# The last six expert units in another order, with the pair tokens gathered earlier and the round count made first

## Chip, cores and metric

The kernel runs on one core of one Trainium2 chip. The metric is the device time of one execution in microseconds. Before the change the median of three runs is 901.22 us (901.0 to 903.43).

## What is computed

One inference step of a two-layer decoder trunk for 288 tokens (256 of a prompt, 32 of running sequences), model width 1024. Layer 0 ends in a dense feed-forward block, layer 1 in a mixture of experts, and only the latter is touched here:

```python
logits = (x @ w_router) + b_router
top_v, top_i = lax.top_k(logits, 2)              # 2 of 8 experts for each token
top_w = jax.nn.softmax(top_v, axis=-1)
gates = sum of one_hot(top_i, 8) * top_w
for e in range(8):
    out = out + gates[..., e:e+1] * swiglu(x, we_gate[e], we_up[e], we_down[e])
# swiglu(x, wg, wu, wd) = (silu(x @ wg) * (x @ wu)) @ wd ; wg, wu: 1024 x 1376, wd: 1376 x 1024
```

## The kernel before, in words

The queue of SyncE (SP) brings the expert weights in. TensorE (PE) multiplies, ScalarE (ACT), VectorE (DVE) and GpSimd (POOL) prepare the operands. Every engine has its own program, written out by hand, and they meet at semaphores.

**Units and steps.** The router counts the tokens of each expert, and the kernel sorts the experts by that count. A *wide* unit is one expert with up to 128 tokens; a *pair* unit is two experts with up to 64 tokens each, side by side. A unit has 27 steps in the order of `STEPS`: eight `up` steps (128 rows of the up matrix each), `gate` 0 to 2 of the **next** unit, eleven `down` steps (the last has 96 rows), then `gate` 3 to 7 of the next unit. The first unit's eight `gate` steps stand ahead of everything (the *lead*, `LEAD = 8`), and the last unit has no gate steps (`LAST_STEPS`). Steps are numbered n = 0, 1, 2, ... through the whole stage.

**Buffers.** Step n uses slot n % 9 (`NSLOT = 9`), so SP may start the load of step n when PE has finished step n - 9 (`w_used`). A slot holds one chunk of a wide step (128 x 1376 or 128 x 1024 fp32) or both chunks of a pair step, which are twice the bytes.

**Wide and pair steps.** A wide chunk is split before use: ACT rounds it to a high half (`moe_high`, L931, five steps ahead of PE), DVE or POOL subtracts that from the raw chunk to get the low half (`moe_low`, four steps ahead; L1699 is DVE's `tensor_tensor`, L757 POOL's), and PE does three passes (L1498, L1499, L1501; for down L1609, L1610, L1613). A pair chunk is used raw, in fp32 (L1514, L1527); ACT and DVE do nothing to it.

**Rounds.** A loop (`Fori(0, more)`) does two wide units a round; `more` is 1 when no expert has over 128 tokens and no later one over 64, else 6. Here it is 1. Behind the loop stand two wide units, then two pair units: in all wide, wide, wide, wide, pair, pair. In this document they are units 0 to 5. `more` comes from `ni_sb`, computed on DVE from the sorted counts; SP, PE, ACT and POOL wait for it (`ni_ready`) before the loop. SP needs it ahead of the load of step 9.

**The lead on DVE.** After the token tables and the gathers' low halves, DVE does `lead_low(r)` and `moe_low` of steps 0 to 3, then the expert ids for the later rounds, the sorted counts and `ni_sb`, then the rest. POOL does `moe_low` of steps 4 and 6 (`POOL_LEAD`).

**Gathers and scatters.** PE gathers tokens into unit order with one-hot matmuls (L1486 to L1489, ten of them for a piece, four pieces). Unit 0 gathers for the next two wide units, unit 2 for all pairs, both between down steps 4 to 9. The results of a unit are scattered back with matmuls (L1544, L1545) between its last gate steps, and DVE adds them to x (L1699 on `xb`).

```python
TOK_ORDER = (2, 4, 0, 3, 5, 1)
NSLOT = 9
STEPS = ([("up", k) for k in range(KT)] + [("gate", 0), ("gate", 1), ("gate", 2)]
         + [("down", k) for k in range(FT)] + [("gate", k) for k in range(3, KT)])
```

Of the kernel before, what the change touches and what calls it, by code (L numbers as in the profile page):

```python
# [15 lines left out]
P = 128  # L16
# [20 lines left out]
FT = 11  # L37
# [54 lines left out]
LEAD_BANK = (3, 5, 4, 6)  # L92
FILL_MASK, FILL_TOK = 11, 6
# [10 lines left out]
SMALL_FROM = LEAD + PER  # L104
POOL_STEPS = (12, 15, 18, 21, 25)
POOL_LEAD = (4, 6)
# [51 lines left out]
def step_of(n):  # L158

    return ("gate", n) if n < LEAD else STEPS[(n - LEAD) % PER]  # L160
# [12 lines left out]
def build(nc, x_d, consts_d, cols_d, misc_d, w_in_d, w_out_d, b_d, c_d, glu_d, ln_d, wst_d, wss_d,  # L173
# [3 lines left out]
    with ctx:  # L177
# [143 lines left out]
        pair_x = [hb[:, 0:1024].rearrange("p (k s) -> p k s", k=KT), stage]  # L321
# [246 lines left out]

        def wait_halves(eng, n, i=None, final=False):
# [12 lines left out]
        def _(sp):  # L582
# [97 lines left out]
            def load_expert_chunk(e, row, n, i=None):  # L680

                r, w = extent(step_of(n))
                if n >= NSLOT:
                    sp.wait_ge(w_used, upto(i, 2 * PER, n - NSLOT + 1))
                sp.dma_start(raw_half(n)[0:r, 0:w], source(e, row, step_of(n))).then_inc(w_in_slot[n % NSLOT], 16)

            def load_small_chunks(experts, step, n, i):

                r, w = extent(step)
                sp.wait_ge(w_used, upto(i, 2 * PER, n - NSLOT + 1))  # L690
                for (e, row), dst in zip(experts, raw_pair(n)):
                    sp.dma_start(dst[0:r, 0:w], source(e, row, step)).then_inc(w_in_slot[n % NSLOT], 16)  # L692
# [16 lines left out]
            def load_pair(i, final):  # L709

                experts = [expert_at(bass.ds(i * 2 + e, 1)) for e in range(2 if final else 3)]
                for n in range(NSLOT, NSLOT + 2 * PER if not final else LEAD + 2 * PER):
                    if final and small_step(n):
                        load_small_chunks(pairs[0], step_of(n), n, i)
                    else:
                        load_expert_chunk(*experts[(n - LEAD) // PER + (step_of(n)[0] == "gate")], n, i)

            with sp.Fori(0, more) as i:
                load_pair(i, False)
            pairs = [[expert_at(slice(4 + 2 * u + g, 5 + 2 * u + g)) for g in range(2)] for u in range(2)]  # L720
            load_pair(more, True)
            n = LEAD + 2 * PER
            for u, steps in enumerate((STEPS, LAST_STEPS)):
                for step in steps:
                    load_small_chunks(pairs[u + (step[0] == "gate")], step, n, more)
                    n += 1
# [8 lines left out]
        def _(pool):  # L735
# [16 lines left out]
            def moe_low(n, i=None, final=False):  # L752

                r, w = extent(step_of(n))
# [124 lines left out]
            for n in POOL_LEAD:  # L879
                moe_low(n)  # L880
# [3 lines left out]
            def pair(i, final):  # L884

                for n in range(LEAD + LOW_AHEAD, LEAD + 2 * PER + (0 if final else LOW_AHEAD)):
                    if moe_by_pool(n) and not (final and small_step(n)):
                        moe_low(n, i, final)

            with pool.Fori(0, more) as i:  # L890
                pair(i, False)
            pair(more, True)
# [14 lines left out]
        def _(act):  # L907
# [19 lines left out]
            def moe_high(n, i=None, final=False):  # L927

                r, w = extent(step_of(n))
# [205 lines left out]

            def one(i, a, final):

                n0 = LEAD + PER * a
                d0 = STEPS.index(("down", 0))
                for q in range(PER):  # L1140
                    if q == 0:
                        gate_silu(i, a, n0)
                    if q == KT and a == 1 and not final:
                        act.wait_ge(w_used, upto(i, 2 * PER, n0 + KT))
                        act.activation(hg_h[1], stage, ACT.Copy).then_inc(hgbh_ready, 1)
                    if q == d0 - 1:
                        hidden_rows(i, a, het_h)
                    if a == 0 and q - d0 in (5, 6, 9, 10):
# [3 lines left out]
                        act.activation((pair_x[0] if final else hg_h[0])[:, 2 * r:2 * r + 2, :],  # L1152
# [3 lines left out]
                    for n in range(n0 + q + ACT_AHEAD - (q == d0 + FT), n0 + q + ACT_AHEAD + (q != d0 + FT - 1)):  # L1156
                        if not (final and small_step(n)):
                            moe_high(n, i, final)

            def pair_unit(i, a, last):  # L1160

                n0, steps = LEAD + PER * a, LAST_STEPS if last else STEPS
                d0 = steps.index(("down", 0))
                gate_silu(i, a, n0)
                hidden_rows(i, a, pair_het)
                output_act(i, a, n0 + d0 + FT)
# [12 lines left out]
            for a in range(2):  # L1179
                one(more, a, True)  # L1180
            for a in (2, 3):
                pair_unit(more, a, a == 3)
# [12 lines left out]
        def _(pe):  # L1195
# [271 lines left out]
            for u, (_, w) in enumerate(TILES):  # L1467
                mm = pe.matmul(ps[:, 7, 24:32], ones[0:w, :], mask[0:w, u, :], start=(u == 0), stop=(u == 2))
# [62 lines left out]
            def scatter(k, i, a, gathers, final=False):  # L1531

                if k == 0:
                    pe.wait_ge(sgt_ready, each(i, a, 1, 1))
                    pe.wait_ge(yel_ready, each(i, a, 2, 1))
                    if gathers:
                        pe.wait_ge(hgh_ready if final else hgl_ready, i * 4 + 8)
# [38 lines left out]
            def one(i, a, final):  # L1576

                n0 = LEAD + PER * a
                gathers = a == 0

                for q, (kind, k) in enumerate(STEPS):
                    if q == 0:
                        pe.wait_ge(xadd, each(i, a, 8, X_MOE - 8 + 3))
                        if a == 0:
                            pe.wait_ge(hgbl_ready, i + 1)
                    if kind == "up":
# [850 lines left out]
```

## Time and profile before

| what | value |
|---|---|
| median of three runs | 901.22 us (901.0 to 903.43) |
| the profiled execution's own time | 900.76 us |
| its span in the trace | 898.9 us |
| mean granted TensorE clock | 0.98 |
| PE, DVE, ACT, POOL busy | 828.6, 561.3, 391.6, 256.3 us |
| HBM read | 197.20 MB |

The trace's times are microseconds from the start of the span, and the profiled execution takes 1.86 us more than its span. The mixture of experts begins at about 490 us and holds the rest of the span. Busy time of PE is modelled: a matmul's record is longer than the distance to the next one, so distances between starts are used for rates.

### The profile page before, as it was taken

To read this page: it belongs to the slowest core of one execution; us is meant where nothing else is said; L and a number is where in the kernel's file an instruction comes from. 1 tells how busy PE (TensorE), PEld (TensorE's weight loads), DVE (VectorE), ACT (ScalarE), POOL (GpSimd) and SP (SyncE) were. 2 spreads that over 40 slices of the span, in tenths; PEclk is the share of its full clock that TensorE was granted. 3 is DMA by queue.
4 is the path that set the end of the run, shared out by engine and by line. 5 is a ranking of instruction groups with operands and counts; after the bars stand their busy time and mean duration, and the time that the engine had idled before them with its cause. 6 is when DMAs were issued, how large, how long until landed. Compare 5 with 4: busy or idle time off the path is not lost.

```text
span 898.9 us, 13791 instructions
## 1 busy us (share of the span) xinstructions
PE 828.6 (92%) x5116; PEld 642.6 (71%) x5116; DVE 561.3 (62%) x978; ACT 391.6 (44%) x574; POOL 256.3 (29%) x208
## 2 busy tenths in 40 slices
PE   9699899999989999999999878999999998868774
PEld 8368679999989999668778766888888652313222
DVE  7959867566955665579733879799987631102004
ACT  5186344455323440486322647767867410001002
POOL 7762124222425540551111205214061320000003
PEclk9989999999999999999999799999999999999998
DMA  9500814655655521820500768999989999999991
GB/s 300 175 1 4 301 58 129 217 167 158 179 142 135 175 72 48 233 104 4 196 1 1 282 260 297 340 312 320 387 291 339 344 406 421 420 374 422 420 390 62
DMA packets 87634, 199.71 MB, mean 222 GB/s; under 512 B 25984, under 2 KB 47728, under 8 KB 87568
## 3 DMA queue, kind: packets, MB, share of 16 engines
q1 hardware_dynamic: 86768, 197.81, 61.8%
q8 instruction: 41, 0.67, 0.3%
q10 hardware_dynamic: 576, 0.59, 0.2%
q0 software_dynamic: 224, 0.43, 0.1%
q14 instruction: 25, 0.20, 0.1%
HBM read 197.20 MB, written 1.61 MB: 221 GB/s over the span
## 4 chain that ended last, share of the span: by engine, by line
PE 56%; DVE 18%; SPq 9%; DMA 7%; issue 5%; ACT 3%; POOL 1%; DVEq 0%; ACTq 0%; POOLq 0%
SPq L692 8%; PE ps L1213 6%; PE ps L1212 6%; PE ps L1214 6%; PE ps L1396 5%; DVE D L1699 4%; DMA wraw_g<-in_moe_w_up 3%; PE ps L1258 3%; PE ps L1501 2%; PE ps L1499 2%; PE ps L1498 2%; DMA wraw_u<-in_moe_w_up 2%; DVE M L1699 2%; PE ps L1609 2%; PE ps L1610 2%
## 5 line engine op out<-in xcount | busy, mean ns | idle before, releaser
L1212 PE MATMUL ps<-Md,split_u 128*128 128x288 f32 (+2 forms) x304 | 89.7, 295 | 0.0
L1214 PE MATMUL ps<-Md,split_u 128*128 128x288 f32 (+2 forms) x304 | 89.1, 293 | 0.0
L931 ACT ACTIVATE wrnd_g<-wraw_g 128x1376 fp32r<-128x1376 f32 (+2 forms) x50 | 60.2, 1214 | 46.0 <-DMA wraw_g<-in_moe_w_down 29.2
L1699 DVE TENSOR_TENSOR xb<-xb,ps 128x288 f32<-128x288 f32 x80 | 33.2, 450 | 67.9 <-PE ps L1396 29.1
L1699 DVE TENSOR_TENSOR wrnd_g<-wraw_g,wrnd_g 128x1376 fp32r<-128x1376 f32 (+1 forms) x42 | 63.0, 1524 | 14.6 <-ACT wrnd_g L931 14.4
L1699 DVE TENSOR_TENSOR wrnd_u<-wraw_u,wrnd_u 128x1376 fp32r<-128x1376 f32 (+1 forms) x38 | 67.7, 1813 | 2.5 <-ACT wrnd_u L931 2.4
L757 POOL TENSOR_TENSOR wrnd_g<-wraw_g,wrnd_g 128x1024 fp32r<-128x1024 f32 (+1 forms) x8 | 29.0, 3631 | 120.0 <-ACT wrnd_g L931 120.0
L763 POOL TENSOR_TENSOR hb<-hb 128x288 f32<-128x288 f32 x11 | 8.7, 795 | 183.3 <-ACT hb L912 182.8
L931 ACT ACTIVATE wrnd_u<-wraw_u 128x1376 fp32r<-128x1376 f32 (+1 forms) x47 | 56.8, 1258 | 3.4 <-DMA wraw_u<-in_moe_w_gate 2.8
L1213 PE MATMUL ps<-hbr,split_u 128*128 128x288 f32 (+1 forms) x192 | 57.1, 297 | 0.0
L1214 PEld LDWEIGHTS ps<-Md,split_u 128*128 128x128 f32 (+2 forms) x304 | 56.9, 187 | 0.0
L1212 PEld LDWEIGHTS ps<-Md,split_u 128*128 128x128 f32 (+2 forms) x304 | 56.8, 187 | 0.1
L925 ACT ACTIVATE split_u<-raw 128x1024 fp32r<-128x1024 f32 (+2 forms) x38 | 39.6, 1048 | 36.4 <-PE ps L1214 36.4
L1699 DVE TENSOR_TENSOR split_u<-raw,split_u 128x1024 fp32r<-128x1024 f32 (+2 forms) x28 | 39.4, 1414 | 19.4 <-ACT split_u L925 19.3
L749 POOL TENSOR_TENSOR split_d<-raw,split_d 128x1024 fp32r<-128x1024 f32 (+1 forms) x9 | 21.4, 2379 | 98.7 <-ACT split_d L925 98.7
L1396 PE MATMUL ps<-D 128*128 128x288 f32 x192 | 48.4, 409 | 0.0
L1212 PE MATMUL ps<-Md,split_d 128*128 128x288 f32 (+1 forms) x144 | 43.4, 301 | 3.9 <-DVE xb L1699 2.8
L1699 DVE TENSOR_TENSOR M<-M,ps 64x256 f32<-64x256 f32 (+3 forms) x38 | 18.3, 504 | 44.0 <-PE ps L1514 43.7
L2186 DVE SCALAR_TENSOR_TENSOR Me<-ps,M,Me 128x512 fp32r<-128x512 f32 x12 | 8.4, 746 | 59.6 <-ACT Me L1173 59.6
L1214 PE MATMUL ps<-Md,split_d 128*128 128x288 f32 (+1 forms) x144 | 42.9, 298 | 0.0
L1396 PEld LDWEIGHTS ps<-D 128*128 128x128 f32 x192 | 36.0, 190 | 9.4
L757 POOL TENSOR_TENSOR wrnd_u<-wraw_u,wrnd_u 128x1376 fp32r<-128x1376 f32 (+1 forms) x9 | 29.4, 3268 | 45.2 <-ACT wrnd_u L931 45.2
(425 smaller groups left out, 2242.8 us busy)
## 6 DMA issues: line engine op xcount, KB each, us to landing
wraw_u<-in_moe_w_gate SPq DMA_DIRECT2D x39, 688.0 KB, 9.2
wraw_g<-in_moe_w_up SPq DMA_DIRECT2D x32, 688.0 KB, 12.9
wraw_g<-in_moe_w_down SPq DMA_DIRECT2D x38, 512.0 KB, 9.3
wraw_u<-in_moe_w_down SPq DMA_DIRECT2D x34, 512.0 KB, 14.0
wraw_u<-in_moe_w_up SPq DMA_DIRECT2D x24, 688.0 KB, 15.1
wraw_g<-in_moe_w_gate SPq DMA_DIRECT2D x18, 688.0 KB, 6.6
raw<-in_ffn_w_gate SPq DMA_DIRECT2D x20, 512.0 KB, 4.5
raw<-in_ffn_w_up SPq DMA_DIRECT2D x20, 512.0 KB, 4.3
```

The lines of the kernel that those rows point to most:

```text
L692: sp.dma_start(dst[0:r, 0:w], source(e, row, step)).then_inc(w_in_slot[n % NSLOT], 16)
L749: pool.tensor_tensor(lo[0:r, 0:w], raw_slot(n)[0:r, 0:w], hi[0:r, 0:w].bitcast(F32), ALU.subtract).then_inc(lo_pool, 1)
L757: pool.tensor_tensor(lo[0:r, 0:w], raw_half(n)[0:r, 0:w], hi[0:r, 0:w].bitcast(F32), ALU.subtract).then_inc(w_lo_pool, 1)
L925: act.activation(split_slot(n)[0][0:r, 0:w], raw_slot(n)[0:r, 0:w], ACT.Copy).then_inc(hi_done, 1)
L931: act.activation(halves(n)[0][0:r, 0:w], raw_half(n)[0:r, 0:w], ACT.Copy).then_inc(w_hi, 1)
L1212: pe.matmul(out, w_hi, x_hi, start=start, stop=False)
L1213: pe.matmul(out, w_hi, x_lo, start=False, stop=False)
L1214: return pe.matmul(out, w_lo, x_hi, start=False, stop=stop)
L1258: mm = pe.matmul(ps[0:n, 4 + t, :], h[:, k, t0:t0 + n], w_in[:, k, 2 * MIX:IN_W], start=(k == 0), stop=(k == KT - 1))
L1396: mm = pe.matmul(bank(out_bank[m]), w_out[:, k, m * P:(m + 1) * P], yn(k), start=(m >= 4 and k == 0), stop=(k == (MT - 1 if m < 4 else KT ...
L1498: pe.matmul(o, hg_h[hg][:, k, :], w_hi[:, f0:f1], start=(k == 0), stop=False)
L1699: return dve.tensor_tensor(o, a, b, op)
```

## The change

Four things change together.

1. The final part is wide, pair, wide, pair in place of wide, wide, pair, pair. With the loop's two wide units the whole is wide, wide, wide, pair, wide, pair. The same chunks are loaded and multiplied, in another order.
2. The pairs' tokens are gathered in unit 2 beside up steps 2 to 5, into banks 6, 7, 0, 1, in place of beside its down steps; their one-hots are made on DVE at that unit's start in place of at its fourth step. The buffer `pair_x[0]` moves.
3. The ids of the first experts are made before the first two token tables, and the later ids, the sorted counts and `ni_sb` before `lead_low(0)`.
4. POOL has no steps of the lead any more: DVE does `moe_low` 4 and 6 too, and the position and gate tables come after steps 8 and 9.

```diff
+PAIR_BANK = (6, 7, 0, 1)
-SMALL_FROM = LEAD + PER
+UNITS = 4
+TOTAL = LEAD + (UNITS - 1) * PER + len(LAST_STEPS)
-POOL_LEAD = (4, 6)
...
-    return n in POOL_LEAD if n < LEAD else (n - LEAD) % PER in POOL_STEPS
+    return n >= LEAD and (n - LEAD) % PER in POOL_STEPS
...
-    return n >= SMALL_FROM and (n >= SMALL_FROM + PER or STEPS[(n - LEAD) % PER][0] == "gate")
+    if n < LEAD:
+        return False
+    a = min((n - LEAD) // PER, UNITS - 1)
+    return (a + (step_of(n, True)[0] == "gate")) % 2 == 1
...
-        pair_x = [hb[:, 0:1024].rearrange("p (k s) -> p k s", k=KT), stage]
+        pair_x = [D[:, 3456:4480].rearrange("p (k s) -> p k s", k=KT), stage]
...
+            def pair_tokens(i, r):
+
+                act.wait_ge(gather_mm, i * 4 + 4 + r + 1)
+                both = ps[:, PAIR_BANK[r], :].rearrange("p (k s) -> p k s", s=2 * P)
+                act.activation(pair_x[0][:, 2 * r:2 * r + 2, :], both[:, :, 0:P], ACT.Copy)
+                act.activation(pair_x[1][:, 2 * r:2 * r + 2, :], both[:, :, P:2 * P], ACT.Copy).then_inc(hgh_ready, 1)
...
-                    pe.matmul(bank(0, P), ones, ones, start=True, stop=True)
+                    pe.matmul(ps[64:128, 1, 0:P], ones[:, 0:64], ones, start=True, stop=True)
...
+                    if final and a == 0 and q - 2 in range(4):
+                        if q == 2:
+                            pe.wait_ge(oh_ready, i + 2)
+                            pe.wait_ge(xadd, each(i, a, 8, X_MOE))
+                        elif q == 4:
+                            pe.wait_ge(esilu_ready, each(i, a, 3, 3))
+                        gather(q - 2, PAIR_BANK[q - 2])
...
-            token_low(0)
-            token_low(1)
             dve.wait_ge(tot_mm, 1)
-            dve.wait_ge(pos_mm, 1)
...
             dve.tensor_copy(ids_sb[:, 0:NE], idf).then_inc(ids_ready, 1)
+            token_low(0)
+            token_low(1)
+            dve.wait_ge(pos_mm, 1)
...
-            for r in range(3):
-                lead_low(r)
-                if not moe_by_pool(r):
-                    moe_low(r)
-            lead_low(3).then_inc(hgbl_ready, 1)
-            moe_low(3)
+            dve.wait_ge(e_ready, 1)
             dve.tensor_copy(ids_sb[:, 8:12], idf[:, 0:4]).then_inc(ids_ready, 1)
...
             dve.tensor_scalar(ni_sb[:, :], cn[:, 2:3], float(MORE), 1.0, ALU.mult, ALU.add).then_inc(ni_ready, 1)
+            for r in range(3):
+                lead_low(r)
+                if not moe_by_pool(r):
+                    moe_low(r)
+            lead_low(3).then_inc(hgbl_ready, 1)
+            moe_low(3)
...
-                    if q == 3 and a == 0:
+                    if a == 0 and q == (0 if final else 3):
```

**Place 1, DVE in the lead.** Before, the round count stands behind the four first chunks (`hbr`, `hgb` are the halves of the gathered tokens, `wrnd_g` a low half, `ids_sb` the expert ids, `ni_sb` the round count):

```order
L2128 SCALAR_TENSOR_TENSOR Me<-ps,G,Me 32x512 [waits tokh_ready]
L1699 TENSOR_TENSOR hbr<-ps,hbr 128x256 [waits hgh_ready]
L1699 TENSOR_TENSOR hgb<-ps,hgb 128x256
L1699 TENSOR_TENSOR wrnd_g<-wraw_g,wrnd_g 128x1376 [waits w_hi]
...
L1699 TENSOR_TENSOR wrnd_g<-wraw_g,wrnd_g 128x1376 [waits w_hi]
L2212 CAST ids_sb<-G 128x4
L2213 CAST ids_sb<-G 128x2
L1699 TENSOR_TENSOR G<-G 128x64
L2215 TENSOR_REDUCE G<-G 128x8 [waits dve_chain]
L2216 TENSOR_SCALAR G<-G 128x1 [waits dve_chain]
L2217 TENSOR_SCALAR G<-G 128x1
L1699 TENSOR_TENSOR G<-G 128x1 [waits dve_chain]
L2219 TENSOR_SCALAR ni_sb<-G 128x1 [waits dve_chain]
```

With the change the same eight instructions stand ahead of the first `hbr`, and the low halves of steps 4 to 8 follow each other:

```order
L2124 SCALAR_TENSOR_TENSOR Me<-ps,G,Me 32x512 [waits tokh_ready]
L2203 CAST ids_sb<-G 128x4 [waits e_ready]
L2204 CAST ids_sb<-G 128x2
L1695 TENSOR_TENSOR G<-G 128x64
L2206 TENSOR_REDUCE G<-G 128x8 [waits dve_chain]
L2207 TENSOR_SCALAR G<-G 128x1 [waits dve_chain]
L2208 TENSOR_SCALAR G<-G 128x1
L1695 TENSOR_TENSOR G<-G 128x1 [waits dve_chain]
L2210 TENSOR_SCALAR ni_sb<-G 128x1 [waits dve_chain]
L1695 TENSOR_TENSOR hbr<-ps,hbr 128x256 [waits hgh_ready]
...
L1695 TENSOR_TENSOR wrnd_u<-wraw_u,wrnd_u 128x1376 [waits w_hi] x4
```

Eight instructions moved past four chunks' low halves and the halves of the gathered tokens, and two low halves (of steps 4 and 6) came to DVE from POOL.

**Place 2, PE in unit 2.** The first wide unit behind the loop, its third up step. Before, it follows the second directly, and nothing but weights is waited for:

```order
L1501 MATMUL ps<-wrnd_g,hbr 128x512 x2
L1501 MATMUL ps<-wrnd_g,hbr 128x352
L572 REGISTER_ALU
L1498 MATMUL ps<-wrnd_g,hbr 128x512 [waits w_lo_dve]
L1499 MATMUL ps<-wrnd_g,hbr 128x512
```

With the change a piece of the gather (`Me` holds the tokens and their one-hots) stands between, and waits for DVE's one-hots and for the last additions to x:

```order
L1507 MATMUL ps<-wrnd_g,hbr 128x352
L1596 REGISTER_ALU
L1597 REGISTER_ALU [waits oh_ready]
L1492 MATMUL ps<-Me 128x256 [waits xadd]
L1493 MATMUL ps<-Me 128x256
L1492 MATMUL ps<-Me 128x256
L1493 MATMUL ps<-Me 128x256
L1495 MATMUL ps<-Me 128x256
```

Four such pieces moved from the down steps to up steps 2 to 5, with a wait for `oh_ready` two steps into the unit. The twelve one-hots it waits for are on DVE:

```order
L1695 TENSOR_TENSOR wrnd_g<-wraw_g,wrnd_g 128x1376 [waits w_hi]
L2316 REGISTER_ALU
L2316 COMPARE_AND_BRANCH
L2266 ISA
L2158 TENSOR_SCALAR Me<-consts,G 128x64 [waits gather_mm]
L2158 TENSOR_SCALAR Me<-consts,G 128x64 x11
```

They stood three low halves later before, and now follow the low half of that unit's fourth up step.

**Place 3, SP's loads behind the loop.** Before, unit 2's gate steps are the next wide expert's (one chunk a step, L685); the program reads, from unit 2's last up chunk on:

```order
L685 DMA wraw_u<-in_moe_w_up 128x1376
...
L685 DMA wraw_u<-in_moe_w_gate 128x1376
...
L685 DMA wraw_d<-in_moe_w_gate 128x1376
...
L685 DMA wraw_g<-in_moe_w_gate 128x1376
```

With the change they are the first pair's, two chunks a step (L705):

```order
L697 DMA wraw_u<-in_moe_w_up 128x1376
...
L705 DMA wraw_u<-in_moe_w_gate 128x1376
...
L705 DMA wraw_u<-in_moe_w_gate 128x1376
...
L705 DMA wraw_d<-in_moe_w_gate 128x1376
...
L705 DMA wraw_d<-in_moe_w_gate 128x1376
```

So the double-sized loads begin one unit earlier, and a wide expert's single ones stand among them later.

## Rows read from the trace of the kernel before

**Rows 1.** The page: busy time of PE; DMA share in 40 slices of the span

```profile
PE 828.6 (92%) x5116; PEld 642.6 (71%) x5116; DVE 561.3 (62%) x978; ACT 391.6 (44%) x574; POOL 256.3 (29%) x208
DMA  9500814655655521820500768999989999999991
```

**Rows 2.** Timeline of SP's queue, 495 to 525: start, us, queue, line, operation

```profile
502.64 0.38 SPq L685 DMA_DIRECT2D wraw_d<-in_moe_w_up  x1
522.52 2.49 SPq L685 DMA_DIRECT2D wraw_g<-in_moe_w_up  x3
```

**Rows 3.** Timeline of DVE, 505 to 600, in the lead

```profile
510.89 1.58 DVE L1699 TENSOR_TENSOR wrnd_g<-wraw_g,wrnd_g 128x1376 fp32r<-128x1376 f32 x1
512.39 3.13 DVE L2212 CAST ids_sb<-G 128x4 int32<-128x4 f32 x1
...
515.50 3.18 DVE L1699 TENSOR_TENSOR G<-G 128x64 f32<-128x64 f32 x1
...
519.41 0.15 DVE L2219 TENSOR_SCALAR ni_sb<-G 128x1 int32<-128x1 f32 x1
```

**Rows 4.** Timeline of POOL, 505 to 600, its two chunks of the lead

```profile
511.45 7.14 POOL L757 TENSOR_TENSOR wrnd_u<-wraw_u,wrnd_u 128x1376 fp32r<-128x1376 f32 x2 [20.81 <-ACT wrnd_u L931]
```

**Rows 5.** Timeline of PE, 508 to 560: lead and unit 0; brackets: idle before, releaser

```profile
512.79 0.39 PE L1498 MATMUL ps<-wrnd_g,hbr 128*128 128x512 f32 x1
...
521.88 0.50 PE L1498 MATMUL ps<-wrnd_u,hbr 128*128 128x512 f32 x1 [4.14 <-DVE wrnd_u L1699]
...
529.17 0.39 PE L1498 MATMUL ps<-wrnd_d,hbr 128*128 128x512 f32 x1
...
534.14 0.50 PE L1498 MATMUL ps<-wrnd_g,hbr 128*128 128x512 f32 x1 [1.08 <-DVE wrnd_g L1699]
...
541.50 0.50 PE L1498 MATMUL ps<-wrnd_u,hbr 128*128 128x512 f32 x1 [1.46 <-DVE wrnd_u L1699]
...
552.69 1.58 PE L1565 MATMUL ps<-consts,M 128*128 128x128 f32 x11 [1.09 <-DVE M L1699]
554.03 0.48 PE L1498 MATMUL ps<-wrnd_g,hgb 128*128 128x512 f32 x1
```

**Rows 6.** Windows: stretch, length, busy times, granted clock, DMA share, GB/s

```profile
522.00:525.00 3.00, 3.00 (x9) 2.49 (x10) 2.76 (x11) 0.00 (x0) 0.00 (x0) 0.56 0.48 128
637.10:691.20 54.10, 54.04 (x282) 46.39 (x281) 46.07 (x57) 39.69 (x46) 17.09 (x5) 1.00 0.93 333
745.60:826.80 81.20, 66.03 (x311) 21.73 (x311) 8.92 (x22) 4.49 (x11) 0.00 (x0) 1.00 1.02 407
800.00:806.00 6.00, 3.59 (x16) 0.77 (x12) 0.00 (x0) 0.00 (x0) 0.00 (x0) 1.00 1.05 256
826.00:860.00 34.00, 28.13 (x138) 9.80 (x138) 4.79 (x13) 2.93 (x7) 0.00 (x0) 1.00 1.02 421
```

**Rows 7.** Timeline of PE: starts of steps in units 0, 2 and 3

```profile
566.12 0.28 PE L1486 MATMUL ps<-Me 128*128 128x256 f32 x1
...
567.30 0.39 PE L1609 MATMUL ps<-wrnd_u,Me 128*128 128x512 f32 x1
...
637.14 0.39 PE L1498 MATMUL ps<-wrnd_d,hbr 128*128 128x512 f32 x1
...
639.01 0.39 PE L1498 MATMUL ps<-wrnd_g,hbr 128*128 128x512 f32 x1
...
691.23 0.39 PE L1498 MATMUL ps<-wrnd_d,hgb 128*128 128x512 f32 x1
...
714.84 0.50 PE L1609 MATMUL ps<-wrnd_g,Me 128*128 128x512 f32 x1
```

**Rows 8.** Timeline of DVE, 626 to 662, around the start of unit 2

```profile
638.51 0.81 DVE L1699 TENSOR_TENSOR xb<-xb,ps 128x288 f32<-128x288 f32 x2
...
645.25 2.04 DVE L2162 TENSOR_SCALAR Me<-consts,G 128x64 fp32r<-128x64 f32 x12
```

**Rows 9.** Timeline, 875 to 900: the last down step and the first scatter

```profile
879.55 2.50 PE L1527 MATMUL ps<-wraw_d,M 96*64 96x512 f32 x8
```

More of the change, by code:

```diff
@@ L707, in _ @@
             more = loops(sp)
[L709 to L716, printed above, removed]
             with sp.Fori(0, more) as i:
-                load_pair(i, False)
+                experts = [expert_at(bass.ds(i * 2 + e, 1)) for e in range(3)]
+                for n in range(NSLOT, NSLOT + 2 * PER):
+                    load_expert_chunk(*experts[(n - LEAD) // PER + (step_of(n)[0] == "gate")], n, i)
+            wide = [expert_at(bass.ds(more * 2 + e, 1)) for e in range(2)]
             pairs = [[expert_at(slice(4 + 2 * u + g, 5 + 2 * u + g)) for g in range(2)] for u in range(2)]
[L721 to L726, printed above, removed]
+            for n in range(NSLOT, TOTAL):
+                a = (n - LEAD) // PER if n < TOTAL - len(LAST_STEPS) else UNITS - 1
+                a += step_of(n, True)[0] == "gate"
+                if a % 2:
+                    load_small_chunks(pairs[a // 2], n, more)
+                else:
+                    load_expert_chunk(*wide[a // 2], n, more, True)
             for k in range(KT):
@@ L878, in _ @@
             pool.wait_ge(tokz_ready, 1)
-            for n in POOL_LEAD:
-                moe_low(n)
             pool.wait_ge(ni_ready, 1)
             more = loops(pool)
[L884 to L888, printed above, removed]
             with pool.Fori(0, more) as i:
-                pair(i, False)
-            pair(more, True)
+                for n in range(LEAD + LOW_AHEAD, LEAD + 2 * PER + LOW_AHEAD):
+                    if moe_by_pool(n):
+                        moe_low(n, i)
+            for n in range(LEAD + LOW_AHEAD, TOTAL):
+                if moe_by_pool(n) and not small_step(n):
+                    moe_low(n, more, True)
             for k in range(1, 4):
@@ L1156, in one @@
                     for n in range(n0 + q + ACT_AHEAD - (q == d0 + FT), n0 + q + ACT_AHEAD + (q != d0 + FT - 1)):
-                        if not (final and small_step(n)):
+                        if not (final and (n >= TOTAL or small_step(n))):
                             moe_high(n, i, final)
[L1160 to L1166, printed above, removed]
+                if len(steps) == d0 + FT:
+                    output_act(i, a, n0 + len(steps))
             def output_act(i, a, used):
@@ L2268, in one @@
                 n0 = LEAD + PER * a
-                d0 = STEPS.index(("down", 0))
-                for q in range(PER):
-                    if q == 3 and a == 0:
+                small, last = final and a % 2 == 1, final and a == UNITS - 1
+                steps = LAST_STEPS if last else STEPS
+                d0 = steps.index(("down", 0))
+                for q in range(len(steps)):
+                    if a == 0 and q == (0 if final else 3):
                         dve.wait_ge(gather_mm, i * 4 + 4)
@@ L2283, in one @@
                         tt(hg_l[1], stage, hg_h[1].bitcast(F32), ALU.subtract).then_inc(hgbl_ready, 1)
-                    if q == d0 - 1:
+                    if q == d0 - 1 and not small:
                         for b in range(3):
@@ L2306, in one @@
                         output_dve(i, a)
-                    if STEPS[q][0] == "gate" and STEPS[q][1] in ADD_AT:
-                        j = 2 * ADD_AT.index(STEPS[q][1])
+                    if steps[q][0] == "gate" and steps[q][1] in ADD_AT:
+                        j = 2 * ADD_AT.index(steps[q][1])
                         for m in (j, j + 1):
```

176 lines of the change are left out of this document (81 added, 95 removed).

## The prediction

> **What bounds the kernel now.** I read the page first. PE is busy 92% of the span, so an average says "PE". The slices say otherwise: DMA share is 8 or 9 from the 25th slice to the last but one, and has a hole at the 21st and 22nd, about where the experts begin [rows 1]. So I took windows, unit by unit [rows 6]. Unit 2, wide, lasts 54.1 us with PE busy 54.0: PE sets the pace, and the queue moves 333 GB/s. Unit 4, a pair, lasts 81.2 us with PE busy 66.0 while DMA share is above 1 at 407 GB/s: the loads set the pace. Where loads run undisturbed they give 421 GB/s (826 to 860) [rows 6]; that is my rate for a full queue. The two kinds of unit have opposite bounds, and nine slots let the queue run nine steps ahead, no more.
>
> Then SP's timeline at the hole: the last of the nine free-slot loads is issued at 502.64, the next at 522.52 [rows 2]. It waits neither for a slot nor for PE: it waits for the round count, which DVE writes at 519.41 [rows 3]. On DVE a cast of 128x4 takes 3.13 us and a 128x64 operation 3.18 us, next to 0.15 us for an operation of like size; POOL's two chunks of the lead run from 511.45 to 518.59, over both [rows 3, 4]. PE idles 4.14 us until 521.88, then has granted clock 0.56 until 525 [rows 5, 6].
>
> **Part 1: the round count and the lead.** The eight instructions go ahead of `lead_low(0)`. Without POOL beside them they are small: from 518.59, where POOL lets go, to 519.56 DVE does five of them, and with two casts of about 0.15 and the 128x64 operation I put them at 1.4 us. DVE had waited there for ACT anyway, so I price them at 0, and at 1.4 for the high end, if that cover is gone.
>
> The low halves then follow each other at 1.50 us (510.89 to 512.39 [rows 3]). Low 3 ends at 512.4; lows 4 to 8, two of them POOL's before, end at 513.9, 515.4, 516.9, 518.4 and 519.9. PE starts step 3 at 512.79 [rows 5] and takes 1.87 us a wide step (637.14 to 639.01 [rows 7]): steps 4 to 7 at 514.66, 516.53, 518.40, 520.27, and unit 0's first up step at 522.14. Each low half is there before. In the trace that step starts at 529.17 [rows 5]: **7.0 us** earlier. The load of step 9 goes out when PE has finished step 0, near 509, not at 522.52, so it is not late.
>
> Up to gate 2 of unit 0 the trace has more waits (1.08, 1.46, 1.09 and smaller ones): 554.03 - 529.17 = 24.9 us for ten wide steps and the transposes, 18.7 + 1.3 = 20.0 at full pace [rows 5]. Some of these 4.9 us go too, as their cause was the late loads. But the position and gate tables, some twenty small instructions (an estimate at 0.15 us each: 3 us), now run on DVE between lows 8 and 10, and DVE at 1.50 us a chunk has only 0.37 us of slack a step. I count 0 here, with -1.5 and +2 as ends. Making the ids ahead of the first two token tables starts the very first loads a little earlier; PE is then at the gathers, so 0.
>
> A rule of the Trainium skill bears on POOL's part. The trace: 3.13 and 3.18 us under POOL, 0.15 us without [rows 3, 4]. SBUF — State Buffer, section "Who interferes with whom", says that DVE and GpSimd share one port pair as an exclusive lock held for a whole instruction, and that casts and two-input operations in SBUF fall under it. By the rule as by the rows the two waits (6 us) vanish; the sum above does not use it, as it counts from each low's end.
>
> **Part 2: the order of units.** I count what the queue still has to load from a point where it becomes continuously busy. At 421 GB/s: wide up or gate (128 x 1376 fp32, 0.7045 MB) 1.67 us, wide down 1.25, pair up or gate 3.35, pair down 2.49. A 96-row pair chunk costs 1.87 plus what the dip at 800 to 806 loses: 256 GB/s for 6 us is 6 x (1 - 256/421) = 2.35 us [rows 6], so 4.2. For a wide one I take 2.1.
>
> While PE does down steps, the queue loads, nine steps ahead, the next gates and ups. Before, these first become pair chunks in unit 3; from its first down step at 714.84 [rows 7] the queue has no more rest. Left then: unit 3: one down, the 96-row one, five pair gates = 20.1; unit 4: 8 up, 3 gate, 10 down, 96-row, 5 gate, all pair = 26.8 + 10.05 + 24.9 + 4.2 + 16.75 = 82.7; unit 5: 26.8 + 24.9 + 4.2 = 55.9. Sum 158.7, end at 873.5. (Landing and PE's last steps bring the last down step to 879.55 [rows 9]; that offset of 6 us is the same after.)
>
> After, the same point comes in unit 2. Unit 2 starts at 637.14. To its first down step it now does what unit 3 does (wide ups, pair gates, 714.84 - 691.23 = 23.6 us), plus four gather pieces of 1.18 us (566.12 to 567.30), 4.7 us, which its down steps lose [rows 7]. Plus a new wait, named next. Left then: 20.1; unit 3 (pair ups, wide gates, pair downs) 26.8 + 5.0 + 24.9 + 4.2 + 8.35 = 69.3; unit 4 (wide ups, pair gates, wide downs) 13.4 + 10.05 + 12.5 + 2.1 + 16.75 = 54.8; unit 5 55.9. Sum 200.1.
>
> *The new wait.* PE wants the one-hots at unit 2's third step, 637.14 + 2 x 1.87 = 640.9. DVE does the last additions to x at 638.51 (0.81), a low half (1.5), then the twelve one-hots (2.04 [rows 8]), and is done at 642.8. PE waits **1.9 us**; behind it on PE stand all up steps, and all wait. Before, the one-hots ran at 645.25, with no one waiting. If DVE is later there, 3 us; if PE is later anyway, 0.
>
> So the point is at 637.14 + 23.6 + 4.7 + 1.9 = 667.4, and the end at 667.4 + 200.1 = 867.5: **6.0 us** ahead of 873.5. Put otherwise: the old order let the queue idle through one more wide unit. Does it really stay busy? It would stop if it got nine steps ahead. In the new unit 4, PE's work and the loads are nearly alike (ups 15.0 to 13.4, pair gates 8.8 to 10.0, downs 15.6 to 14.6); PE enters it some 7 us behind (first wide chunk after a pair one goes through ACT and DVE, about 3 us; five wide gates with scatters, 11.4 us of PE for 8.4 of loads). 8 us of lead is at most six chunks. It holds, with little to spare: I give this term 3 to 8 us.
>
> **Sum.** 7.0 + 6.0 = 13.0 us off 900.76 us of the profiled execution (span 898.9) gives 887.8 us; the median 901.22 stands 0.5 us above that execution, so I forecast **888.2 us**. Part 4 of the change, the moved buffer and the filler matmuls of 64 columns, moves no work: 0.
>
> **Rivals.**
> - *Only the lead gains.* The wide units behind pair units are late for the split, PE falls back, and the slots fill, so that the queue idles as before. For it: the thin margin in unit 4. Against it: PE's idle share in unit 4 of before, 15 of 81 us [rows 6]. Time: 900.8 - 7.0 + 0.5 = 894.2. Chance 0.12.
> - *Only the order gains.* In unit 0 DVE becomes the bound (two more lows, the tables, the loop's own one-hots) and gives back the 7 us before the loop's second unit. Time 895.2. For it: DVE's waits in rows 5 are of that kind. Against it: POOL no longer holds it for 6 us. Chance 0.08.
> - *Nothing of either* (a load elsewhere is the true bound): 0.04, within 0.3% of 901.2.
> - *Slower: PE loses its clock.* The row: after 4.14 us of idling, clock 0.56 (the 1.2 GHz level, for most of 3 us) [rows 5, 6]. The new order has a place with two waits close together, at the end of unit 3's downs: about 2 us for the 96-row chunk, then about 3 us for the first split. If the clock fell there and at the like places, and pair steps then ran at 1.2 GHz, a pair step would take 4.9 us of PE for 3.35 us of loads: 1.5 us lost a step, and from nine such steps on the 13 us are gone; all 16 up steps of units 3 and 5 would give 888.2 + 24 = 912. Against it: clock 1.00 all through unit 4 of before, at waits of 0.8 us a step [rows 6]. Chance 0.04. The Trainium skill speaks for it: TensorE: Matmul & The Clock Gate, section "HAM oscillation", tells of a kernel that waits for DMA between short bursts and is throttled again at each. The 1.00 of unit 4 does not bear that out for waits this short.
> - My forecast: 0.72.
>
> **Range.** The bounds: 5.5 to 9 us for the lead, 3 to 8 for the order, so 884.2 to 892.7 for the likeliest case alone; with both one-sided rivals, **884.0 to 895.3**. Faster by over 0.3%: 0.92; within 0.3% (what a measurement of this kernel can tell from no change): 0.04; slower: 0.04.
>
> **What would show it.** `ni_sb` written near 503 on DVE; SP's tenth load near 509; first up step near 522; no granted clock below 0.9 between 510 and 875; a PE wait of 1.9 us for DVE's one-hots near 634; loads at about 421 GB/s with no gap from about 660; in unit 3 a wait of 2 to 3 us at the first wide gate; the last down step near 866.5. I am wrong if the queue has gaps in the last 200 us, if DVE is ahead of PE by nothing in unit 0, or if PE's clock drops at unit 3's end.

## The result

The changed kernel takes **892.61 us** (median of four runs, 891.37 to 894.31) against 901.14 us (901.0 to 903.43) for the kernel before, run beside it: a ratio of 0.9901 with a 95% interval of 0.9878 to 0.9923. That is 8.5 us or 1.0% faster. I had forecast 888.2 us, a gain of 13.0. The time lies inside the range of 884.0 to 895.3, but a third of the gain is missing.

The profiled execution took 892.68 us, its span is 890.9 us. From its page, PE's busy time and clock and the DMA share in 40 slices; they answer to [rows 1]:

```profile
PE 827.4 (93%) x5116; PEld 643.5 (72%) x5116; DVE 559.9 (63%) x980; ACT 391.4 (44%) x574; POOL 243.9 (27%) x206
PEclk9889999999999999999999699999999999999998
DMA  9500723755554521830500697989979999989991
```

Each slice is 22.3 us. Behind the hole, the 24th slice (512 to 535 us) now has a DMA share of 9 in place of 6. But the 36th (780 to 802 us) has an 8 inside the last stretch of nines, where I had expected no gap. And PE's clock is 0.6 in the 23rd (490 to 512 us), where it was 0.7.

The lead, on SP's timeline (answers to [rows 2]) and DVE's (answers to [rows 3]):

```profile
501.87 0.39 SPq L697 DMA_DIRECT2D wraw_d<-in_moe_w_up  x1
510.59 5.92 SPq L697 DMA_DIRECT2D wraw_g<-in_moe_w_up  x4
```

```profile
503.03 0.17 DVE L2203 CAST ids_sb<-G 128x4 int32<-128x4 f32 x1
...
503.18 0.22 DVE L1695 TENSOR_TENSOR G<-G 128x64 f32<-128x64 f32 x1
...
504.12 0.15 DVE L2210 TENSOR_SCALAR ni_sb<-G 128x1 int32<-128x1 f32 x1
...
513.31 6.09 DVE L1695 TENSOR_TENSOR wrnd_u<-wraw_u,wrnd_u 128x1376 fp32r<-128x1376 f32 x4
```

`ni_sb` is written at 504.12 in place of 519.41, the cast takes 0.17 us in place of 3.13, and SP's tenth load goes out at 510.59 in place of 522.52. Now PE's timeline; the rows are the first filler group, the first up step of unit 0, the transposes, unit 2's start, the new wait for the one-hots, unit 2's first down step, and the last down step (they answer to [rows 5, 7, 9]):

```profile
489.42 4.28 PE L1469 MATMUL ps<-ones_r 128*64 128x128 f32 x22
...
523.32 0.39 PE L1504 MATMUL ps<-wrnd_d,hbr 128*128 128x512 f32 x1
...
544.78 1.58 PE L1571 MATMUL ps<-consts,M 128*128 128x128 f32 x11 [1.09 <-DVE M L1695]
...
628.91 0.39 PE L1504 MATMUL ps<-wrnd_d,hbr 128*128 128x512 f32 x1
...
634.68 0.38 PE L1492 MATMUL ps<-Me 128*128 128x256 f32 x1 [1.87 <-DVE Me L2158]
...
659.46 0.50 PE L1633 MATMUL ps<-wrnd_g,Me 128*128 128x512 f32 x1
...
872.09 1.89 PE L1533 MATMUL ps<-wraw_d,M 96*64 96x512 f32 x8
```

Read it from the two ends. Unit 2 starts 8.2 us earlier than before (628.91 against 637.14 [rows 7]). The last down step starts 7.5 us earlier (872.09 against 879.55 [rows 9]), and the span is 8.0 us shorter. So **all of the gain is there when unit 2 starts, and the order, which acts from there on, brought nothing** in this execution. My sum had 7.0 us for the lead and 6.0 for the order.

Where the order's 6 us went shows in the windows (stretch, length, busy times of PE, PEld, DVE, ACT, POOL, granted clock, DMA share, GB/s):

```profile
740.00:750.00 10.00, 7.15 (x26) 1.90 (x24) 0.00 (x0) 0.02 (x1) 0.00 (x0) 0.83 1.03 289
780.00:790.00 10.00, 10.00 (x55) 4.53 (x54) 7.58 (x10) 8.01 (x11) 3.73 (x2) 1.00 0.85 326
790.00:800.00 10.00, 10.00 (x46) 8.17 (x45) 9.61 (x7) 4.59 (x5) 5.03 (x3) 1.00 0.89 293
800.00:810.00 10.00, 10.00 (x48) 5.65 (x47) 1.41 (x2) 1.26 (x2) 1.88 (x1) 1.00 1.02 420
```

The 289 GB/s at 740 is the 96-row pair chunk that I had priced. The 326 and 293 are new: against 420 they are (94 + 127) / 42 = 5.3 us of a resting queue, in unit 4. What it waits for stands on SP's and PE's timelines:

```profile
785.64 0.33 SPq L697 DMA_DIRECT2D wraw_d<-in_moe_w_down  x1
789.45 0.33 SPq L697 DMA_DIRECT2D wraw_g<-in_moe_w_down  x1
```

```profile
786.74 2.53 PE L1520 MATMUL ps<-wraw_g,D 128*64 128x512 f32 x12
789.20 0.50 PE L1633 MATMUL ps<-wrnd_g,Me 128*128 128x512 f32 x1
```

Down load 8 goes out at 789.45, when PE has finished gate 2 (786.74 to 789.20), whose slot it takes. The queue is nine steps ahead, and issues nothing for 3.5 us.

### The profile page after: what moved, and what is told of

It is laid out like the page before. It is cut to its first block, busy times and chain, and to the rows that moved or that the text cites. A ratio compares the mean times of both kernels' runs of the same rounds, so it can differ in the third digit from the quotient of the medians.

```text
span 890.9 us, 13793 instructions
## 1 busy us (share of the span) xinstructions
PE 827.4 (93%) x5116; PEld 643.5 (72%) x5116; DVE 559.9 (63%) x980; ACT 391.4 (44%) x574; POOL 243.9 (27%) x206
## 4 chain that ended last, share of the span: by engine, by line
PE 63%; DVE 15%; DMA 6%; ACT 5%; issue 5%; SPq 4%; POOL 1%; DVEq 0%; ACTq 0%; POOLq 0%
PE ps L1219 6%; PE ps L1218 6%; PE ps L1220 6%; PE ps L1402 5%; SPq L705 4%; PE ps L1520 4%; DMA wraw_u<-in_moe_w_gate 4%; DVE D L1695 3%; PE ps L1507 3%; PE ps L1505 3%; PE ps L1504 3%; PE ps L1633 2%; PE ps L1634 2%; PE ps L1637 2%; DVE M L1695 2%
## 5 line engine op out<-in xcount | busy, mean ns | idle before, releaser
L1695 DVE TENSOR_TENSOR wrnd_u<-wraw_u,wrnd_u 128x1376 fp32r<-128x1376 f32 (+1 forms) x40 | 72.2, 1838 | 25.6 <-ACT wrnd_u L935 25.4
L765 POOL TENSOR_TENSOR wrnd_g<-wraw_g,wrnd_g 128x1024 fp32r<-128x1024 f32 (+1 forms) x8 | 23.5, 2942 | 136.6 <-ACT wrnd_g L935 136.6
L1219 PE MATMUL ps<-hbr,split_u 128*128 128x288 f32 (+1 forms) x192 | 57.1, 297 | 0.0
L765 POOL TENSOR_TENSOR wrnd_u<-wraw_u,wrnd_u 128x1024 fp32r<-128x1024 f32 (+1 forms) x7 | 22.1, 3163 | 116.7 <-ACT wrnd_u L935 116.7
L1520 PE MATMUL ps<-wraw_u,D 128*64 128x512 f32 (+1 forms) x192 | 40.4, 555 | 5.0 <-DMA wraw_u<-in_moe_w_up 5.0
L1219 PEld LDWEIGHTS ps<-hbr,split_u 128*128 128x128 f32 (+1 forms) x192 | 35.9, 187 | 0.1
```

The costliest lines, as they stand in the source:

```text
L765: pool.tensor_tensor(lo[0:r, 0:w], raw_half(n)[0:r, 0:w], hi[0:r, 0:w].bitcast(F32), ALU.subtract).then_inc(w_lo_pool, 1)
L1219: pe.matmul(out, w_hi, x_lo, start=False, stop=False)
L1520: mm = pe.matmul(ps[own, b0 + b, 0:f1 - f0], pair_x[u][:, k, own], w[g][:, f0:f1], start=(k == 0), stop=(k == KT - 1))
L1695: return dve.tensor_tensor(o, a, b, op)
```

## The experiments

Twelve kernels ran, in three sets of four, each set on one chip with the kernel before beside it (medians 900.96, 901.79 and 901.5 us). Single executions of one kernel differ by 5 us and more, so beside each median I give the ratio to the kernel before, and in the traces I compare stretches.

### The order alone, the lead alone

```diff
 # e1_order_only: the changed kernel, its lead taken back
+            for n in POOL_LEAD:
+                moe_low(n)
...
+            lead_low(3).then_inc(hgbl_ready, 1)
+            moe_low(3)
             dve.tensor_copy(ids_sb[:, 8:12], idf[:, 0:4]).then_inc(ids_ready, 1)
 # e2_lead_only: the kernel before, with the changed lead (no lows on POOL); units and pairs as they were
```

> The changed kernel with the lead of the kernel before: round count after the lows, POOL_LEAD lows, 128-column filler matmuls. So this is the order alone. Theory A (the order is worth nothing and the lead all): from the start of unit 2 on both kernels took the same time (244.9 and 245.1 us), so this run ties with the kernel before, 901 us (899 to 903), unit 2 starts near 637 us of its span and the last down step some 242.5 us later. Theory B (my prediction's: the order is worth 6 us less the 0 that the lead lost): 895 us. In both the profile should show SP's load of step 9 late again, near 522 us.

> The kernel before, its units in their old order, with the new lead: round count, number casts and one-hots made before the lows, no lows on POOL in the lead, and the 64-column filler matmuls with the total in bank 0. Theory A: the lead is worth the 8.2 us that unit 2 starts earlier in the changed kernel, and the old order keeps them: 893 us (891.5 to 894.5), the same as the changed kernel. Theory B: 7.0 us of 13 come from the lead, and the order's share was then eaten by something else that the changed order brought: also near 893 us if the lead is 8 us, so it is the run of the order alone that tells the two apart; above 897 us both theories are wrong, since then lead and order need each other.

Order alone: 899.6 us (897.92 to 903.13, twelve runs), ratio 0.9983 (0.9958 to 1.0007). Lead alone: 893.1 us (891.37 to 895.82), ratio 0.9899 (0.9857 to 0.9941), as fast as both together. Theory A (the lead is all) holds, theory B (6 us of order) falls: the interval leaves the order at most 3.8 us and is centred on 1.5. In the profile of the order alone SP's tenth load is late again (525.60, in an execution that came to the fillers 2.7 us later than the kernel before), TensorE waits the same 1.87 us for the one-hots, and the queue rests in unit 4 as well, at 312 and 286 GB/s in two windows of 10 us, 5.8 us.

### Which part of the lead

Two parts of the new lead can be had alone: the early round count with POOL's lows kept (L1's candidate), and POOL's two lows given to DVE with the count left where it was (L2's).

```diff
 # e5_count_early: kernel before, DVE's part and the second filler group as changed, but
             for n in range(4, LEAD + LOW_AHEAD):
-                moe_low(n)
+                if not moe_by_pool(n):
+                    moe_low(n)
 # e6_no_pool_lead: kernel before, one line
-POOL_LEAD = (4, 6)
+POOL_LEAD = ()
```

> The kernel before, in its old order, with the round count and the one-hots early as in the changed kernel, but POOL keeps its two lows of the lead (steps 4 and 6, 7.14 us for both). Theory L1 (the round count's place gives the 8 us: it is out before POOL starts its lows, so nothing waits behind them): SP's next load near 511 us in place of 522.5, and 893.5 us. Theory L2 (the lows on POOL cost by themselves, since VectorE's small operations or TensorE's steps 4 and 6 wait for them wherever the count stands): not under 896 us.

> The kernel before with POOL's two lows of the lead given to VectorE and nothing else: the round count stays behind the lows of steps 0 to 3. Its casts then take 0.2 us in place of 3.13 and 3.18 us, the count is out at 513.6 us of the span in place of 519.4, SP's next load is at 516.7 us in place of 522.5, and the first up step, which waited 4.14 us, is bound by TensorE's own queue of work: 5.8 us of the queue's delay gone, of which 4.1 us reach the end. Forecast 896.8 us by theory L1. By theory L2 it gives nearly all of the 8: 893 us.

Count early: 894.67 us, ratio 0.993 (0.9907 to 0.9953); SP's next load goes out at 507.51. That is nearer to L1's 893.5 than to L2's "not under 896". No lows on POOL: 894.82 us, ratio 0.9921 (0.9901 to 0.9941). Each alone brings 6 to 7 us, both 8 to 9: they remove the same stall, and are not to be added. My price for the second, 896.8 us, was wrong: I took 4.1 us as all that the path could give. But with the casts at 0.17 us DVE does its lows of the lead earlier too, and PE had been waiting for those [rows 5]. From the totals' matmuls to unit 0's transposes the profiles give 60.3 us before, 53.6 with the count early, 51.4 without POOL's lows, 51.2 for the changed kernel and 51.1 for the lead alone. The lead alone is the early count without POOL's lows, so POOL's lows cost 2.5 us of the stretch where the count is early (53.6 to 51.1), and once they are gone the early count adds 0.3 us (51.4 to 51.1), which is less than profiles differ by: the nine with the changed lead give 49.0 to 51.3. First DVE with the count early, then POOL in the same stretch:

```profile
509.41 1.58 DVE L1700 TENSOR_TENSOR wrnd_g<-wraw_g,wrnd_g 128x1376 fp32r<-128x1376 f32 x1
510.91 9.01 DVE L1700 TENSOR_TENSOR wrnd_u<-wraw_u,wrnd_u 128x1376 fp32r<-128x1376 f32 x2
519.85 1.58 DVE L1700 TENSOR_TENSOR wrnd_d<-wraw_d,wrnd_d 128x1376 fp32r<-128x1376 f32 x1
```

```profile
509.52 8.95 POOL L757 TENSOR_TENSOR wrnd_u<-wraw_u,wrnd_u 128x1376 fp32r<-128x1376 f32 x2 [19.59 <-ACT wrnd_u L931]
```

Two of DVE's lows, 1.58 us each when alone, take 9.01 us beside POOL's two. Two engines did four lows in 9 us; DVE alone does four in 6.09 (`x4` at 513.31 above). Taken one by one, the four end in turn: POOL at 513.99, DVE at 515.44, POOL at 518.48, DVE at 519.93. From POOL's end to DVE's are 1.45 us, about one of DVE's lows alone, and from DVE's end to POOL's 3.0: by these times they run one behind the other. The Trainium skill (SBUF — State Buffer, section "Who interferes with whom") tells of a port pair that DVE and GpSimd lock for whole instructions; this trace agrees.

### Fillers and clock

In the changed kernel's profile the first filler matmuls (64 columns) took 4.28 us, before (128 columns) 2.70, and the totals behind them were late. I took the width for the cause.

```diff
 # e3_fill_wide
-            fill(FILL_MASK)
+            for _ in range(FILL_MASK):
+                pe.matmul(bank(0, P), ones, ones, start=True, stop=True)
```

> The changed kernel with its first eleven filler matmuls on 128 columns into bank 0, as in the kernel before, so that only the second group is on 64 columns. Theory A: the 64-column matmuls let the granted clock fall to 0.50 at 490 to 493 us, and the totals came 1.2 us late for it; here the granted clock stays at 1.00 there, the totals come at 492.4 us, the first up step at 522.1 us, and the time is 1.2 us less: 891.4 us. Rival: the 1.2 us come from the mask being late and not from the clock; then the totals stay at 493.6 us and the time at 892.6 us.

> The changed kernel once more, untouched, on the same chip as the other three of this set, so that they can be compared with it directly: 892.6 us within 1 us. The granted clock beside its first filler matmuls (64 columns) shows whether the 0.50 at 490 to 493 us comes back: it was 0.50 in two profiles of such fillers and 1.00 in one, so that column count alone does not set it.

With wide fillers: 891.35 us, ratio 0.9887 (0.9843 to 0.993); clock 1.00 there. That fitted. But the untouched kernel, profiled again (median 891.48 us of seven, ratio 0.9891, 0.9877 to 0.9906), had its 64-column fillers at full clock, and a kernel with the wide ones (the late gathers with wide fillers, below) had the fall:

```profile
489.60 2.62 PE L1469 MATMUL ps<-ones_r 128*64 128x128 f32 x22
```

```profile
490.00:494.00 4.00, 4.00 (x22) 4.00 (x23) 2.35 (x19) 3.12 (x6) 0.95 (x1) 0.57 0.02 4
```

Over all fourteen profiles the group took about 4.3 us in three of six with 64 columns, and in two of eight with 128. The same instructions behind the same work fall to the 1.2 GHz level in some executions and not in others. My theory is refuted: the width alone does not decide. One fall costs about 1.4 us (4.2 us from the first filler to the totals in place of 2.8 or 2.9), and is a part of the spread.

### The new wait for the one-hots

```diff
 # e4_gather_late; e8_wide_late has e3's edit as well
-                    if final and a == 0 and q - 2 in range(4):
-                        if q == 2:
+                    if final and a == 0 and q - 4 in range(4):
+                        if q == 4:
...
-                        gather(q - 2, PAIR_BANK[q - 2])
+                        gather(q - 4, PAIR_BANK[q - 4])
```

> The changed kernel with the pairs' gathers beside up steps 4 to 7 of the third unit in place of 2 to 5, so that the pairs' one-hots are made when the first gather comes. Theory A: TensorE's wait of 1.87 us for them goes, but nothing of it is left at the end, since the queue meets its nine-slot limit in units 4 and 5 and the pair steps run at the queue's pace: 892.6 us. Rival: that wait delays all that follows, and its removal brings 1.9 us: 890.7 us. The start of the fourth unit (690.26 us now) against the start of the last down step (872.09 us now) tells where it is lost.

> The changed kernel with both mends together: the first eleven filler matmuls on 128 columns, and the gathers beside up steps 4 to 7. Theory A: the wait of 1.9 us for the pairs' one-hots goes to the end undiminished (the run with the late gathers alone was at 889.2 us) and the filler adds up to 1.2 us where its clock had fallen: 888.5 us. Rival: the time of the late gathers alone was luck of its spread, and this one comes to 891 us.

Late gathers: 889.23 us, ratio 0.9847 (0.98 to 0.9893); one of its six executions took 1174.83 us at a mean granted clock of 0.65, which no profile explains, and is left out. With the wide fillers: 890.88 us, ratio 0.9873 (0.9855 to 0.989), 1.6 us below the changed kernel's on the same chip by ratio. In both profiles the wait is gone, and unit 1's to unit 2's transposes take 55.0 and 55.4 us in place of 57.1 and 58.7 in the changed kernel's two profiles; in the second of these the clock fell to 0.50 for 2 us behind the wait. Whether the 1.9 us reach the end is not shown. For it: from unit 1's transposes to the last down step it is 270.3 and 272.7 us (269.7 in a third kernel without the wait, below), in place of 273.6 and 271.8. Against it: the intervals of the two kernels run on one chip overlap, their medians are 0.6 us apart (890.88 and 891.48), and the run with both mends came where its rival, "luck of its spread", had it, at 891 and not at 888.5.

### TensorE's work in units 3 and 4, and the hand-overs

If PE is late in unit 4 and the queue therefore rests, less work for PE should let the queue run.

```diff
 # e7_thin_unit4, in gate_or_up
-                for b, (f0, f1) in enumerate(FCH):
+                for b, (f0, f1) in enumerate(FCH if not (final and hg == 1) else ()):
                     mm = pe.matmul(ps[:, b0 + b, 0:f1 - f0], hg_l[hg][:, k, :], w_hi[:, f0:f1],
 # e9_hold: e8, and in one(), ahead of a gate step
+                        if small and not last and k in (0, 3):
+                            for _ in range(HOLD[k // 3]):
+                                pe.matmul(bank((0, 5)[k // 3], P), ones, ones, start=True, stop=True)
```

> The changed kernel, but unit 4's expert leaves out the third of its gate and up matmuls that multiplies the tokens' low parts (16 steps, 48 matmuls of the 144; its output is less exact). That takes 16 x 0.65 = 10 us of TensorE's work out of units 3 and 4 and no byte out of the queue. Theory A (TensorE is late in unit 4, so that it frees the nine slots too late and the queue pauses for 5.3 us at 780 to 800 us): the pause goes, and the time falls by about those 5 us, to 887.5 us, no more, since then the queue's bytes bound it. Theory C (what the order lost, it lost in the waits for data at the hand-overs from pair to wide, where TensorE waits for the transfer and the rounding): the time falls by at most 1 us, to 891.6 us or more.

> The same two mends, and at both hand-overs from pair to wide in unit 3 (before its gate steps 0 and 3) eight more filler matmuls of 128x128, each group about 2 us, put where TensorE waits 2.2 and 1.8 us for the rounded weights. If the clock that falls after those waits (0.53 to 0.61 at 718 to 722 us, 0.50 at 746 to 748 us) costs what the slow first wide step shows (3.5 us in place of 2.1), it is kept at full speed and the time is 1 to 1.5 us less than without them: 887.3 us. Rival: the steps after a hand-over run at the queue's pace all the same, and the time is unchanged or up to 1 us more, where the fillers last longer than the wait.

Thin: 892.15 us, ratio 0.9898 (0.9876 to 0.992), beside 0.9891 for the untouched kernel. Ten us of PE work less, and no gain: theory A's 887.5 falls, and the time is in theory C's bound of 891.6 or more. The queue still rests, 331 and 349 GB/s in the same two windows, 3.8 us. PE's and SP's timelines of this kernel show why:

```profile
783.85 1.58 PE L1574 MATMUL ps<-consts,M 128*128 128x128 f32 x11 [2.72 <-DVE M L1698]
785.36 1.08 PE L1523 MATMUL ps<-wraw_g,D 128*64 128x512 f32 x4
```

```profile
781.32 0.33 SPq L697 DMA_DIRECT2D wraw_d<-in_moe_w_down  x1
788.08 3.29 SPq L697 DMA_DIRECT2D wraw_g<-in_moe_w_down  x3
```

PE is ready sooner and then waits 2.72 us for DVE's product, with gate 2 behind the transposes in its program. That slot comes free at 788, and the queue issues nothing for 6.4 us. Why the product is late stands on ACT's and DVE's timelines (`M` is the product):

```profile
780.88 1.06 ACT L935 ACTIVATE wrnd_g<-wraw_g 128x1024 fp32r<-128x1024 f32 x1 [9.92 <-DMA wraw_g<-in_moe_w_down]
```

```profile
781.97 1.23 DVE L1698 TENSOR_TENSOR wrnd_g<-wraw_g,wrnd_g 128x1024 fp32r<-128x1024 f32 x1 [6.41 <-ACT wrnd_g L935]
783.12 1.71 DVE L1698 TENSOR_TENSOR M<-M,ps 128x512 f32<-128x512 f32 x3
```

In DVE's program the product stands behind the low half of a down chunk, and that chunk, the first that ACT rounds after a pause of 9.92 us, has only just come in. So the free slot waits here for a chain that begins with the queue's own load: load, high half, low half, product, transposes, gate 2. Less work for PE does not shorten that. The changed kernel has the same order, with the product from 783.56 to 785.27, ready just as PE comes to its transposes at 785.39. Whether the product ahead of that low half would let the queue run, no run tried.

The hand-over with fillers in the wait: 889.1 us, ratio 0.986 (0.9841 to 0.988). PE's wait of 2.16 us at the first wide gate is filled and the step behind it is at full speed. At the second hand-over the clock fell all the same (0.50 at 746 to 750 us), behind a wait of 3.20 us for the load before it. It is the fastest of the four run beside each other in that set, 1.8 us under the same kernel without these fillers and by the ratios 2.8 us under the changed kernel (0.9891, 0.9877 to 0.9906). Both pairs of intervals overlap, so that a version that beats both kernels is likely here and, against the changed one, not shown. The fall of the clock at that hand-over is again not in every execution: with the same wait before it, the windows of the changed kernel in its two profiles are

```profile
718.00:722.00 4.00, 3.90 (x11) 3.27 (x12) 4.00 (x9) 1.45 (x2) 0.00 (x0) 0.57 1.02 418
```

```profile
715.00:719.00 4.00, 2.84 (x12) 2.18 (x13) 4.00 (x9) 1.81 (x2) 0.00 (x0) 1.00 1.02 419
```

From unit 2's transposes to unit 3's it is 67.9 us with the fall and 66.2 without; with the fillers it is 66.4. So they can save at most a fall that comes in some executions only, and the step gains nothing by them where it does not come.

### Eight steps ahead in place of nine

Theory D: the limit of nine slots is what takes the order's gain.

```diff
 # e11_eight_new, e12_eight_old: loads of the last four units
-                    sp.wait_ge(w_used, upto(i, 2 * PER, n - NSLOT + 1))
+                    sp.wait_ge(w_used, upto(i, 2 * PER, n - NSLOT + (2 if final else 1)))
```

> The changed kernel, in whose last four units the queue may be at most eight steps ahead of TensorE in place of nine (each load waits for one more step; no byte and no TensorE work changes). Theory D (the order's gain is lost since the queue fills its nine slots beside the wide units and cannot save up for the pairs; each change from wide to pair loads therefore starts with only nine steps in hand): one step less in hand costs one wide load, 1.7 us, at each of the two changes of this order: 892 + 3.4 = 895.4 us. Theory C (only the hand-overs' waits and the clock behind them took the gain): no change, 892 us.

> The kernel before with the same limit of eight steps ahead in its last four units. Its order changes from wide to pair loads once. Theory D: 1.7 us, 901.2 + 1.7 = 902.9 us, half of what the new order loses by it. Theory C: no change, 901.2 us.

New order: 895.8 us, ratio 0.9931 (0.991 to 0.9952), 3.6 us over the untouched changed kernel by the ratios, as theory D had it, and against theory C's 0. Old order: 904.85 us, ratio 1.0036 (1.0021 to 1.0051), 3.35 us more, double my 1.7. So the ninth slot is worth about 3.5 us in either order. The limit binds, but my count of one wide load for each change to pairs does not explain the old order's price. In the old order's profile each of the three stretches from unit 2's transposes to unit 5's is 2.0 to 2.3 us longer (57.3, 67.7 and 78.2 us in place of 55.2, 65.4 and 76.1), so that the price is not paid at the change alone. Why the two are alike stays open, and as both orders pay, this pair of runs does not show that the limit is what took the order's gain.

## Why the prediction was right and wrong

**Place and kind of the gain.** Right: the load of step 9 waited for the round count, and DVE was held behind POOL. Both vanished as described. The experiments add that the two are one stall: either mend alone brings 6 to 7 us.

**Lead, 7.0 us.** Mis-sized by a little, on the low side: 8.2 us at unit 2, though this execution lost 1.2 us to a clock fall in the fillers. What I had put at 0 from the first up step to gate 2 (24.9 us before) shrank by 2.1: gate 2 starts at 546.12, and 546.12 - 523.32 = 22.8 us, of 20.0 at full pace. The first up step came at 523.32, forecast 522.14; the 1.2 us are the fillers'. In the repeated profile without the fall it is at 522.13.

**One-hot wait, 1.9 us.** Right: 1.87 us, 634.68. Down step 0 came 30.55 us after unit 2's start, forecast 30.2.

**Fillers and moved buffer, 0.** Right, after a detour: the slow fillers were an accident of the execution.

**Order, 6.0 us.** This is the step that failed: "Does it really stay busy?", "It holds, with little to spare." It does not hold, and behind unit 2's start the two profiles of the changed kernel are 0.7 us longer and about 1 us shorter than the one before, the order alone brought 1.5 us, and I had given it 3 to 8. From unit 2's first down step to the last down step I forecast 206.1 us; the profile has 212.6, the repeated one 209.3 (657.98 to 867.30). In each profile of the new order that I read for it the queue rests in unit 4, for 4.8 to 5.8 us. I had compared PE's work and the loads over the whole of unit 4 and found them alike, ups 15.0 to 13.4, downs 15.6 to 14.6. But a queue that can be nine steps ahead does not average over 27: behind the ups come the product, the transposes and two pair gates with nothing to free a slot quickly, while eight cheap down loads (1.25 us) fill what is free. That this rest is what took the 6 us is read from the traces; no run took the rest away. Nor does it give the excess exactly: it is 6.5 us in one profile with a rest of 5.3, and 3.2 in the other with 4.8, where other parts came 1.6 us shorter for a cause that I did not find. Falls of the clock make most of the 3.3 us between the two: 1.7 us at the hand-over, and 1.9 us in the last stretch (27.5 in place of 25.6 us from unit 5's transposes to the last down step, with a clock of 0.80 at 870 to 875 us in place of 1.00).

The rival "only the lead gains" (0.12; 894.2) was the true case or near it: with the lead at 8.2 it gives 893.0, measured 892.6. It had half of the mechanism, "the slots fill, so that the queue idles as before", but not because "PE falls back": with 10 us less of PE's work the queue rests all the same. That the time lies inside my range is luck of the sum: its two low ends, 5.5 and 3 us, add to the 8.5 us that in fact the lead gave nearly alone.

**Slower through the clock.** The fall came at the place named (0.57 after a wait of 2.16 us), but cost 1.7 us once, not 1.5 a step, and not in every execution. My sign "no granted clock below 0.9 between 510 and 875" failed with it.

What stays open: what more slots would give, or the product ahead of the down chunk's low half, as no run tried either, and why the old order loses as much by one slot less.

## What to carry to other kernels

When two kinds of work with opposite bounds are mixed, don't compare sums over a unit: walk the queue's lead step by step against the number of slots, ask at each place where it would fill them, and follow what frees the next slot through every engine: here it went back to the queue's own load. A term that "holds, with little to spare" is a coin, not a term, and deserves the rival's chance. And before moving an instruction out of a stall, look for what makes it long: here giving POOL's two lows to DVE, one line, brought about as much as the whole rearrangement of the lead.

## What the hardware showed unexpectedly

POOL's help can be negative: DVE's low of 128x1376 takes 1.58 us alone and 4.5 beside a POOL low, as the two run in turn, so that four lows on both engines took 9.0 us and on DVE alone 6.1. The granted clock falls or not, in executions of one and the same kernel, at the same instructions: 4.28 or 2.62 us for the same fillers, 0.57 or 1.00 behind a wait of 2.16 or 2.15 us. A single profile's clock is no evidence on an edit; it took a second profile of the untouched kernel to see that.
